# Transposed gate and up products in a mixture-of-experts layer: 128-column weight pieces stationary, tokens moving

## What is computed

```
def routed_experts(xf, idx, wts, wg, wu, wd):
    ...
        xb = xf[tok]                          # rows of tokens of one expert
        hid = jax.nn.silu(xb @ wg[e]) * (xb @ wu[e])
        yb = (hid @ wd[e]) * w[..., None]
        acc = acc.at[tok].add(yb)
```

## Time and profile before

| | |
|---|---|
| three timed executions | 2062.09, 2062.33, 2065.42 us |
| profiled execution, span from first to last instruction | 2064.1 us (the page gives no other time of it) |
| PE busy | 1995.9 us (97%) |
| DVE / POOL / ACT busy | 1138.1 / 774.3 / 504.3 us |
| gate and up products L3164 | 1056 records, 470.5 us |
| down products L3180 | 528 records, 237.6 us |
| transposes of hid L3172 | 132 records, 26.2 us |
| expert weights | 66 x 3 transfers of 1 MB |
| TensorE clock granted, mean | 0.989 of full |

### The profile page before, as it was taken

The page is one execution under the profiler, slowest core; times in us unless marked ns, Lnnn a source line. Parts: engine busy times, 40 slices in busy tenths (PEclk is TensorE's granted clock), DMA queues, the critical chain, the costliest instruction groups (busy, mean ns, idle before and its releaser), DMA issues.

```text
span 2064.1 us, 23702 instructions
## 1 busy us (share of the span) xinstructions
PE 1995.9 (97%) x7237; PEld 1014.8 (49%) x7238; DVE 1138.1 (55%) x3065; ACT 504.3 (24%) x1102; POOL 774.3 (38%) x717
## 2 busy tenths in 40 slices
PE   8999999999999999999999999999999999999991
PEld 6444667575544444444445554444444444444440
DVE  6222546776611222335676656966666666666645
ACT  3111554452322222214432230111111111111113
POOL 1762005612122222115980002554545545545531
PEclk9999999999999999999999999999999999999996
DMA  5421000011132222144253006999999999999974
GB/s 147 132 87 41 21 21 22 22 47 47 46 130 75 72 82 77 57 124 167 101 203 144 38 31 258 341 356 348 349 356 352 358 361 350 352 352 354 353 238 168
DMA packets 129639, 370.45 MB, mean 179 GB/s; under 512 B 33712, under 2 KB 65668, under 8 KB 103832
## 3 DMA queue, kind: packets, MB, share of 16 engines
q1 hardware_dynamic: 103960, 314.83, 40.8%
q0 software_dynamic: 23520, 54.61, 10.9%
q10 hardware_dynamic: 2080, 0.01, 0.1%
HBM read 320.57 MB, written 68.17 MB: 188 GB/s over the span
## 4 chain that ended last, share of the span: by engine, by line
PE 46%; POOL 3%; DVE 2%; issue 2%; DMA 1%; ACT 0%; SPq 0%; DVEq 0%; POOLq 0%
PE banks L3164 22%; PE banks L3180 10%; PE banks L2288 4%; PE banks L2335 3%; POOL arena L2136 2%; PE banks L2014 2%; PE banks L279 1%; PE banks L2351 1%; PE banks L2776 1%; PE banks L3172 1%; PE banks L2311 1%; DMA arena<-in_w_router_dram 0%; DVE arena L3240 0%; DVE arena L3157 0%; PE banks L2298 0%
## 5 line engine op out<-in xcount | busy, mean ns | idle before, releaser
L3164 PE MATMUL banks<-arena 128*128 128x512 f32 x1056 | 470.5, 598 | 3.1 <-DVE arena L3157 0.7
L3143 POOL DMA_INDIRECT arena<-h_rows,index x268 | 276.7, 1032 | 142.1 <-issue 73.6
L3164 PEld LDWEIGHTS banks<-arena 128*128 128x128 f32 x1056 | 195.8, 190 | 227.2 <-issue 225.8
L1720 PE MATMUL banks<-arena 128*128 128x512 f32 x672 | 299.0, 594 | 1.5 <-ACT arena L323 1.5
L3180 PE MATMUL banks<-arena 128*128 128x512 f32 x528 | 237.6, 592 | 1.3 <-ACT arena L2979 0.8
L3151 POOL DMA_INDIRECT sums<-arena,row_to x66 | 108.0, 1636 | 274.5 <-DMA sums<-arena,row_to 255.6
L3157 DVE STREAM_TRANSPOSE arena<-arena 128x1024 f32<-128x1024 f32 x66 | 133.9, 2028 | 134.3 <-PE banks L3164 134.3
L279 PE MATMUL banks<-arena 128*128 128x512 f32 x416 | 193.5, 602 | 2.2 <-PEq L108 2.2
L1720 PEld LDWEIGHTS banks<-arena 128*128 128x128 f32 x672 | 123.1, 190 | 136.1 <-issue 133.9
L3127 DVE TENSOR_SCALAR index<-row 32x1 uint32<-32x1 f32 x1072 | 155.4, 145 | 17.1
L3180 PEld LDWEIGHTS banks<-arena 128*128 128x128 f32 x528 | 100.2, 190 | 127.0 <-issue 125.3
(11 more groups left out here) (400 smaller groups left out, 2428.9 us busy)
## 6 DMA issues: line engine op xcount, KB each, us to landing
arena<-in_w_exp_gate_dram SPq DMA_DIRECT2D x66, 1024.0 KB, 9.1
arena<-in_w_exp_up_dram SPq DMA_DIRECT2D x66, 1024.0 KB, 11.2
arena<-in_w_exp_down_dram SPq DMA_DIRECT2D x66, 1024.0 KB, 18.1
arena<-in_w_in_dram SPq DMA_DIRECT2D x26, 1024.0 KB, 5.4
gates<-arena SPq DMA_DIRECT2D x60, 256.0 KB, 2.0
arena<-gates SPq DMA_DIRECT2D x15, 1024.0 KB, 7.6
arena<-h_rows,index POOLq DMA_INDIRECT x268, 7.9
arena<-in_x_dram SPq DMA_DIRECT2D x8, 512.0 KB, 5.6
```

Of the source, the lines that this page charges most:

```text
L1720: mm = pe.matmul(gate_bank(n, b), left[:, k, :], right[:, k, :], start=(alone and k == 0), stop=(k == 3), skip_group_check=True)
L3143: return pool.indirect_dma_start(w.x[k][:, 256 * q:256 * (q + 1)], None, rows, bass.IndirectOffsetOnAxis(ap=g.index[:, k, q:q + 1], axis=0 ...
L3164: mm = pe.matmul(g.bank[:, 2, :].rearrange("p (a f) -> p a f", a=2), xT[:, k, :], wgu[:, :, k, :], start=(k == 0), stop=(k == KT - 1))
```

## The change

The gate and up products are made transposed. Stationary is now a 128-column piece of the weights (every second hidden column, because the down weights lie so that hidden column 2n+j is on partition n, piece j), and the 128 tokens move. The result in the PSUM bank is hidden columns x tokens: four pieces of 128 x 128, gate 0, gate 1, up 0, up 1. Each needs 8 matmuls over the features, 32 in all instead of 8. Silu and the product work on this layout, and their result is directly what the down products want as stationary operand. So `turn_hid` on TensorE and the copy on ScalarE go, with their semaphores. `hidT` has two buffers, since it is now written while the down products of the block before read theirs; the product waits for the down products of two blocks before. The "rest" loop changes alike.

```
-    for k in range(KT):
-        mm = pe.matmul(g.bank[:, 2, :].rearrange("p (a f) -> p a f", a=2), xT[:, k, :], wgu[:, :, k, :],
-                       start=(k == 0), stop=(k == KT - 1))
-    return mm
-
-
-def turn_hid(g, pe, hid):
-    cols = hid.rearrange("p (n k) -> p k n", k=2)
-    for k in range(2):
-        mm = pe.transpose(g.bank[:, 3, k * P:(k + 1) * P], cols[:, k, :], g.ident[:])
+    for a in range(2):
+        for f in range(2):
+            out = g.bank[:, 2, (2 * a + f) * P:(2 * a + f + 1) * P]
+            for k in range(KT):
+                cols = wgu[:, a, k, :].rearrange("p (n j) -> p j n", j=2)
+                mm = pe.matmul(out, cols[:, f, :], xT[:, k, :], start=(k == 0), stop=(k == KT - 1))
     return mm
...
             def down(i, c):
-                pe.wait_ge(s["hTr"], val(i, c) + 1)
+                pe.wait_ge(s["hid"], val(i, c) + 1)
                 wait(pe, s["ya"], val(i, c))
                 wait(pe, s["yb"], val(i, c))
...
                     first.last_down()
-                turn_hidden(i, c)
...
             def hidden(i, c):
                 dve.wait_ge(s["silu"], val(i, c) + 1)
-                wait(dve, s["hT"], val(i, c))
-                dve.tensor_tensor(w.hid, w.silu, bank[:, 2, FF:], ALU.mult).then_inc(s["hid"], 1)
+                if has(i, c, -2):
+                    dve.wait_ge(s["down"], val(i, c) - 1)
+                dve.tensor_tensor(w.hidT[c % 2].rearrange("p k n -> p (k n)"), w.silu, bank[:, 2, FF:],
+                                  ALU.mult).then_inc(s["hid"], 1)
...
-            def hidden(i, c):
-                act.wait_ge(s["hT"], val(i, c) + 1)
-                wait(act, s["down"], val(i, c))
-                act.activation(w.hidT.rearrange("p k n -> p (k n)"), bank[:, 3, 0:FF], ACT.Copy).then_inc(s["hTr"], 1)
...
-    w.silu, w.hid, w.hidT = g.region(LISTS + 2048, FF), g.region(LISTS + 2048 + FF, FF), take(2, P)
+    w.silu = g.region(LISTS + 2048, FF)
+    w.hidT = [take(2, P), g.region(LISTS + 2048 + FF, 2, P)]
```

More of the change, by code:

```diff
@@ L2683, in experts @@
     first = norm_and_route(g, w, joint)
-    names = "q lst list flag row idx xT up silu hid hT hTr down ya yb to tables tabled places".split()
+    names = "q lst list flag row idx xT up silu hid down ya yb to tables tabled places".split()
     s = {n: sem("e_" + n) for n in names}
-    more = "places q lst list flag row idx xT up silu hid hT hTr down ya yb to gathered stored free used".split()
+    more = "places q lst list flag row idx xT up silu hid down ya yb to gathered stored free used".split()
     v = {n: sem("v_" + n) for n in more}
@@ L2784, in up, with down @@
                 up_products(g, pe, w.xT, c % 4).then_inc(s["up"], 1)
-            def turn_hidden(i, c):
+            def down(i, c):
                 pe.wait_ge(s["hid"], val(i, c) + 1)
-                wait(pe, s["hTr"], val(i, c))
-                turn_hid(g, pe, w.hid).then_inc(s["hT"], 1)
-            def down(i, c):
-                pe.wait_ge(s["hTr"], val(i, c) + 1)
                 wait(pe, s["ya"], val(i, c))
@@ L2795, in down @@
                 ends = isinstance(i, int) and val(i, c) == NB - 1
-                down_products(g, pe, w.hidT, c % 4).then_inc(v["down"] if ends else s["down"], 1)
+                down_products(g, pe, w.hidT[c % 2], c % 4).then_inc(v["down"] if ends else s["down"], 1)
             def before():
@@ L2830, in _ @@
                 pe.wait_ge(v["hid"], o + 1)
-                turn_hid(g, pe, w.hid).then_inc(v["hT"], 1)
-                pe.wait_ge(v["hTr"], o + 1)
                 pe.wait_ge(v["ya"], o + 1)
                 pe.wait_ge(v["yb"], o + 1)
-                down_products(g, pe, w.hidT, 1).then_inc(v["down"], 1)
+                down_products(g, pe, w.hidT[1], 1).then_inc(v["down"], 1)
                 pe.matmul(bank[0:1, 0, 8:9], g.ident16[:, 0:1], g.ident16[:, 0:1],
@@ L2958, in _ @@
                 dve.wait_ge(v["silu"], o + 1)
-                dve.tensor_tensor(w.hid, w.silu, bank[:, 2, FF:], ALU.mult).then_inc(v["hid"], 1)
+                dve.tensor_tensor(w.hidT[1].rearrange("p k n -> p (k n)"), w.silu, bank[:, 2, FF:],
+                                  ALU.mult).then_inc(v["hid"], 1)
                 dve.wait_ge(v["free"], o + 2)
@@ L2997, in step @@
                     result(i, c - 1)
-                hidden(i, c)
             count = []
@@ L3008, in _ @@
                 act.activation(w.silu, bank[:, 2, 0:FF], ACT.Silu).then_inc(v["silu"], 1)
-                act.wait_ge(v["hT"], o + 1)
-                act.activation(w.hidT.rearrange("p k n -> p (k n)"), bank[:, 3, 0:FF], ACT.Copy).then_inc(v["hTr"], 1)
             act.wait_ge(v["to"], 4 * count[0])
```

## The result

The changed kernel takes 2073.65 us (median of 4 runs, 2073.58 to 2076.44), the kernel before beside it 2063.43 (4 runs, 2062.09 to 2065.42): a ratio of 1.0051, interval 1.0038 to 1.0063. That is 10 us slower, where 2060 was forecast and 2072 was the upper end. The profiled execution is the one of 2076.44, with a span of 2074.7; another had 2073.58 with a span of 2071.8.

What follows compares the result with a forecast made beforehand. TensorE at 11.06 us a block bounds the kernel, with transfers at 11.2 taking over once TensorE needs 10.76; only 2.0 us at start and end remain, so 2062.3 - 2.0 = 2060.3, say 2060, range 2042 to 2072.

Steps and rivals of the forecast that it cites:

- Gate and up products: TensorE, each block: 64 records at 0.109 us make 7.0 us against 6.94 before, so +0.06 us.
- two readings: Strided weight loads in gate and up products: either the stride costs nothing (taken), or 55 ns are added to every load.
- Transposes and lists: TensorE after the down products: two transposes gone, -0.23 us a block; lists no longer behind the wait for `hid`, -0.13.
- The sum: TensorE's terms together: -0.3 us a block, giving 10.76 us, between -0.55 and +0.1.
- The end: Last blocks and rest loop: TensorE ends 2.5 to 3.5 us earlier, last scatter at most 2.5; 2.0 taken with the start.
- The new wait: Next gate and up products wait for `hid` themselves; 0.9 us to spare, so priced at nothing.
- What is late next: Expert blocks: after some 16 blocks products wait for their weights, and transfers set the pace at 11.2 us a block.
- rival B: Faster: transfers are elastic and follow TensorE, 18 us over 61 blocks and 2.0 at the end, 2042; chance 0.13.
- A: The forecast itself: transfers hold the pace, 2060 us, own range 2056 to 2065; chance 0.62.
- no idle before block 64's down products: Sign that the forecast is right: the 0.82 us wait for the copy before block 64's down products disappears.
- C: Slower: the strided load keeps its matmuls at 0.115 to 0.12 us, 2065 to 2084, 2072 at 0.117; chance 0.12.
- D: Much slower: strided load's 55 ns come on top, 0.164 us a record, 2273; doubled, 0.218 and 2501; chance 0.13.

Runs made afterwards that it cites:

- g1: The changed kernel with only 64 of the 128 tokens moving in the gate and up products, stationary step of two kept: 2078.37 us.
- g2: The changed kernel with contiguous stationary weight pieces and only 64 of the 128 tokens moving in the gate and up products: 2081.17 us.
- e1: The changed kernel with contiguous stationary weight pieces instead of every second column, meeting the wrong down-weight rows: 2065.89 us, 1.0008 of the kernel before.
- f2: The changed kernel loading only 256 of 2048 floats per partition of the down weights from the fifth block on: 2072.75 us, 1.0036 of the kernel before.
- e4: The changed kernel with gate and up products as before (16 records of 512 columns), still without transposes and copy: 2064.56 us, 1.0003 of the kernel before.
- light transfers: Only 256 of 2048 down-weight floats per partition loaded from the fifth block on; added to e1 2049.90 us, added to e4 2031.67 us.
- e2: e1 with down weights loaded to fit, in runs of 4 KB instead of 8, so the full computation is done: 2070.78 us, 1.0034 of the kernel before.

## Why the prediction was wrong

**Gate and up products: the step that failed.** "64 x 0.109 = 7.0 us" is 64 x 0.119 = 7.62 us: +0.68 a block in place of +0.06. Two errors lie in it. The first is the floor. 0.109 is what 128 columns need by the 0.116 of 136 columns, and the floor beside it was read as 0.107, just under it. But the row of 64 columns was misread: its first two matmuls start 0.056 us apart, and all the rest 0.1117. So the floor of a contiguous load is 0.112, which lies over the 0.109, and halving the columns (g1, g2) shows that at 64 and at 128 columns the load sets the beat. That is 0.28 us a block (7.22 of e1 against 6.94).

The second error is the stride: from two readings the one at no cost was taken. The stride accounts for 0.119 - 0.113 a record, 0.4 us a block, as e1 shows. The support that the prediction named, a spacing of 0.115, is no spacing: it is half of the 0.23 us from the first transpose to the lists. In the trace the two strided transposes start 0.109 to 0.110 us apart in 62 of 66 blocks, and contiguous transposes do the same:

```profile
30.88 3.66 PE L739 MATMUL banks<-ident,arena 128*128 128x128 f32 x32
```

That is (3.66 - 0.27) / 31 = 0.109 a record. So two strided transposes in a row showed no price of the stride, although their loads take 196 ns against 141. They have one record each where a matmul has two, and the other float32 matmuls with such stationary sizes load 190 ns. The rows before had no long stream of strided loads, and the step took these pairs for one.

**Transposes and lists: right in kind, 0.12 us too small.** The gap from the down products to the next products is 0.21 us in every block. Before it was 11.06 - 6.94 - 3.43 = 0.69 on average. That is -0.48 a block, where -0.23 - 0.13 = -0.36 was forecast. It lies in the larger half of the stated bounds. That the wait for `hid` had held back what stood behind it is argued and not shown, as the transposes and their wait went together in every kernel. In the blocks written out the transposes of the kernel before waited 1.47 us for `hid` at 1303.81, and the lists and products still followed 0.34 and 0.21 us apart; so if the wait held something back, it was in the hardware loop. The copy on ScalarE had cost nothing in the loop, as said.

**The sum** is then +0.68 - 0.48 = +0.20 in place of -0.3, the 11.26 against 11.06 of the blocks' starts. Corrected in the first term alone, the forecast's own working gives +0.68 - 0.36 = +0.32 a block, over its 61 blocks 20 us, less its 2.0: about 2080, past the 2073.65 measured. With both terms as measured it is 12 us less 2.0, so 2072.5. That the 2.0 fits here is in part luck, as said below under "The end".

In the pair of profiles the 10.6 us are made up otherwise: 12 us for the blocks, less 3.6 for the stall and the slow products behind it, and 2.6 more for the one wait at 1352.05, which is 11. The changed kernel's other three executions are 2.8 us shorter than the profiled one, which would fit one without that wait; they have no trace.

**The new wait, "costs nothing": right in the loop of the changed kernel, wrong for a faster one.** From 1365 to 1940 TensorE waits for nothing. Among the first blocks the products do wait for `hid`, 0.88 us at 1292.02 and 1.76 at 1352.05 (0.94 and 0.18 in f2). In e4 they wait 29 times in 400 us, as the last link behind the scatters. The prediction counted what `hid` takes when nothing delays VectorE, not what stands ahead of it on VectorE.

**What is late next: right in kind, not used here.** The changed kernel does not wait for the transfers (share 0.99, 350 GB/s), and rival B's elastic transfers and A's held pace could not be told apart in it. e1 and e4 do: 0.2 and 0.5 us a block taken off TensorE gave nothing (1.0008 and 1.0003), where the same tables gave 14 and 32 us with light transfers. B falls. Which wait shows the full transfers is not the same in every kernel. In e1 and e4 it is not the one that was named: results wait for scatters to land. In e2 it is the named one: the products wait for the down weights. In g2 both stand side by side: the products wait four times for the down weights (2.6 us), and 15 results on ScalarE wait for scatters (82.0 us), between 1400 and 1950. g2 makes the same transfers as e1, so what decides between the two is open.

**The end, -2.0 us: only in part borne out.** It was put together from the 3 us by which the stall and the slow products had set the last blocks back, 0.3 less for each of these blocks, block 64's shorter wait, and 0.97 in the last chain. The stall and the slow products did go, 3.6 us. The rest did not come. The two blocks before block 64 take 11.05 and 10.97 us in the changed kernel, where they took 10.61 and 10.52 before: the mis-sized term again, 0.4 more each. Block 64's down products still wait, now 0.94 us for VectorE's result (the row at 2018.21) in place of 0.82 for the copy, so the sign "no idle before block 64's down products" did not come. The last chain is 0.30 us shorter, not 0.97. e1 and e4, where TensorE was faster and the transfers held the pace, come out 2.5 and 1.1 us above the kernel before, which is no difference, but not 2 below.

**The rivals and the range.** It went as C said in kind: a strided load keeps its matmuls at 0.119, and TensorE is never idle in the loop. C's sum at 0.119 would be 7.62 + 3.43 + 0.35 = 11.40 a block, about 2081, too high because it counts 0.35 for the lists where 0.21 was measured. C decides from 0.114, only 0.002 over the true floor, and the loads of 196 ns against 141 were on its side. The one row that spoke for C by name, 0.115, was misread, and so was what was said against it. With the floor misread as well, C looked farther off than it was. A chance of 0.12 cut the range at 2072, inside C's own span of 2065 to 2084. D's price in series (0.164) fell with e1.

No version beat both. e2, which does the whole computation with contiguous loads, is 3 us below the changed kernel and 7 above the one before. The light kernels say what would have to come first: fewer bytes, before any matmul saved here is worth anything. Whether fewer scatters would do it too was not tried.

## What to carry to other kernels

Price a small float32 matmul by its stationary load, at the step that the load has, and do not scale it by the moving columns up to 128; if a long row of that very load is in the trace, take the spacing of its starts as the price, record by record, and not the first gap or a row of two. Where an engine and the transfers run within 2% of each other, the two directions are worth different amounts: time taken off the engine goes into waits (0 of 32 us here), time put on it is paid in full where the engine had no idle time. A doubtful term then belongs on its dear side, and the range must reach over all of the rival that it decides.

## What the runs showed of the hardware that was not expected

- A load of 128 x 128 float32 and its matmul of 64 or 128 columns take 0.112 us contiguous and 0.118 at a step of two floats; with 128 columns it is 0.175 at three, 0.235 at four and 0.240 at eight. The loads' own durations (196 ns at step two in the changed kernel, 192 contiguous in e1) do not tell this.
- Full transfers can show first in the landing of the indirect scatters with addition, which follow one another (e4: results wait 261.4 us on ScalarE in 400), and not in that of the weights. In e2 it was the weights, in g2 both.
- Behind waits of 1.8 to 1.9 us the products of one block took longer: 9.30 us for 7.78 in the changed kernel, 9.01 for 7.39 in e2, as the 8.81 for 7.11 of the earlier trace rows. The granted clock over the 9 us at 1352 was 0.81 in the mean, a mixture of its two levels, and 1.00 in the next block:

```profile
1352.00:1361.00 9.00, 8.95 (x63) 8.98 (x64) 4.77 (x23) 0.00 (x0) 4.96 (x5) 0.81 0.99 342
1364.00:1372.00 8.00, 8.00 (x71) 7.47 (x70) 4.95 (x23) 0.69 (x1) 3.47 (x3) 1.00 0.80 293
```

  Two waits close together did the same: 0.55 and 1.16 us in e1 before products of 8.82 at 1962.11, 0.80 and 1.01 in e4 before products of 8.70 at 1966.20. Single waits of 0.4 to 0.8 us in e1 and e4 left the durations as they were, and so did one of 1.61 in e4 at 1304.47 (7.11).
- Down weights in runs of 4 KB instead of 8 KB cost 5 us over the kernel (e2 against e1), at the same DMA share (1.00) and 350 GB/s instead of 355 over 1400 to 1950.
